# Gated feed-forwards on one core: up-projections as two by two blocks with seven products

## What is computed

```python
D_FF = ((8 * D_MODEL // 3 + 127) // 128) * 128        # 2816
def swiglu_ffn(h, w_in, w_out):                       # w_in 1024 x 5632, w_out 2816 x 1024
    gate, up = jnp.split(h @ w_in, 2, axis=-1)
    return (jax.nn.silu(gate) * up) @ w_out
# in each layer: x = x + 0.5 * swiglu_ffn(rms_norm(x, g), ...), at the start and at the end
```

## Time and profile before

| what | value |
|---|---|
| median of 3 runs | 2511.85 us (2510.24 to 2515.91) |
| the profiled execution's own time | 2515.61 us |
| its span, first to last instruction | 2513.8 us |
| mean granted TensorE clock | 0.982 |
| TensorE busy (matmul) | 2414.4 us, 96% |
| VectorE busy | 588.0 us, 23% |
| ScalarE busy | 356.4 us, 14% |
| matmuls of line 1966 (up) | 615.9 us |
| matmuls of line 1980 (down) | 308.6 us |

### The profile page before, as it was taken

One profiled execution on the slowest core, in us unless ns is written; L12 is line 12 of the kernel. 1 busy time (PEld: TensorE's weight loads), 2 busy tenths in 40 slices (PEclk: granted clock), 3 DMA queues, 4 the chain that ended last, 5 costly groups with the idle time before them and its releaser, 6 DMA issues. The chain is left out here.

```text
span 2513.8 us, 29170 instructions
## 1 busy us (share of the span) xinstructions
PE 2414.4 (96%) x12476; PEld 1658.3 (66%) x12476; DVE 588.0 (23%) x1204; ACT 356.4 (14%) x668; POOL 44.1 (2%) x75
## 2 busy tenths in 40 slices
PE   7999979999999899999999999999999999999998
PEld 4778744444444577778676677777777867667775
DVE  2888221111111200022551110010002164211001
ACT  1123121111111100012213110000001221311000
POOL 1000000000000100000000000000000000000000
PEclk8999979999999999999999999999999999999999
DMA  9565649999999644452322144444445232214442
GB/s 382 222 261 224 240 104 376 422 421 422 422 423 422 232 139 155 157 189 100 131 89 101 51 143 150 151 167 134 150 151 214 76 141 106 95 55 144 150 150 84
DMA packets 176135, 499.46 MB, mean 199 GB/s; under 512 B 7193, under 2 KB 99625, under 8 KB 146097
## 3 DMA queue, kind: packets, MB, share of 16 engines
q1 hardware_dynamic: 172224, 481.23, 51.0%
q0 software_dynamic: 3680, 16.43, 2.2%
q10 hardware_dynamic: 144, 0.52, 0.1%
HBM read 491.34 MB, written 6.82 MB: 198 GB/s over the span
## 5 line engine op out<-in xcount | busy, mean ns | idle before, releaser
L1966 PE MATMUL bank<-xT,ring 128*128 128x256 f32 x2816 | 615.9, 379 | 0.0
L1966 PEld LDWEIGHTS bank<-xT,ring 128*128 128x128 f32 x2816 | 535.1, 190 | 87.9 <-issue 17.2
L1980 PE MATMUL bank<-ring,fh 128*128 128x512 f32 x704 | 308.6, 592 | 0.0
L1980 PEld LDWEIGHTS bank<-ring,fh 128*128 128x128 f32 x704 | 133.8, 190 | 151.3 <-issue 149.2
L2620 DVE TENSOR_TENSOR fs<-bank,R 128x512 f32<-128x512 f32 x44 | 30.4, 692 | 771.1 <-PE bank L1966 771.1
L2015 PE MATMUL bank<-xT,ring 128*128 128x256 f32 x704 | 152.6, 379 | 0.0
L835 PE MATMUL bank<-xT,ring 128*128 128x256 f32 x640 | 143.8, 385 | 2.8 <-ACT xT L279 2.8
L2015 PEld LDWEIGHTS bank<-xT,ring 128*128 128x128 f32 x704 | 133.4, 190 | 18.0
L2418 ACT ACTIVATE fs<-fs 128x512 f32<-128x512 f32 x44 | 27.7, 630 | 800.9 <-DVE fs L2620 800.9
L835 PEld LDWEIGHTS bank<-xT,ring 128*128 128x128 f32 x640 | 122.9, 193 | 22.0 <-ACT xT L279 2.9
L1370 PE MATMUL bank<-ring,xg 128*64 128x512 f32 x512 | 114.4, 594 | 7.6 <-DMA ring<-in_w 7.6
(11 more groups left out here) (433 smaller groups left out, 2215.1 us busy)
## 6 DMA issues: line engine op xcount, KB each, us to landing
ring<-in_w SPq DMA_DIRECT2D x128, 1024.0 KB, 18.6
ring<-in_ffn_w_in SPq DMA_DIRECT2D x88, 1024.0 KB, 7.7
ring<-in_first_pieces SPq DMA_DIRECT2D x33, 2048.0 KB, 12.2
more<-in_w SPq DMA_DIRECT2D x64, 1024.0 KB, 19.7
ring<-in_ffn_w_out SPq DMA_DIRECT2D x44, 1024.0 KB, 4.9
ring<-in_w_mix_in SPq DMA_DIRECT2D x12, 2048.0 KB, 8.8
ring<-in_xattn_w_kv SPq DMA_DIRECT2D x8, 2048.0 KB, 10.5
ring<-in_w_mix_out SPq DMA_DIRECT2D x4, 2048.0 KB, 9.7
```

The lines of the kernel that those rows point to most:

```text
L1966: last = nc.tensor.matmul(bank[2 * par + u][:, c * SEQ:(c + 1) * SEQ], w[:, k, m:m + P], xT[:, k, :], start=(k == 0), stop=(k == KD - 1))
L1980: last = nc.tensor.matmul(bank[4 + 2 * half + t][:, :], fh[:, par, c * SEQ + t * P:c * SEQ + (t + 1) * P], w[:, c, half * 512:(half + 1) * ...
```

## The change

The two by two block form of the product: with x cut into two halves of tokens by two halves of the inner dimension, and the 512 columns of a weight piece cut into gate and linear half by the same halves of the inner dimension, seven block products in place of eight give the result, at the price of sums of blocks of x (4, once a feed-forward, into `Sx`), sums of weight blocks (4 a group, into `Tw`) and sums of products (7 a group, into `part` and `whole`). Each product is 4 matmuls of 128 x 128 by 256 columns. This holds for the groups 1 to 10; group 0 (`up_first`) is the plain product as 16 matmuls of 512 columns.

x is now the stationary operand, so the hidden values come out with the token on the partition. The scale by 1/rms is then a number per partition in ScalarE's silu, and `R`, `spread_rstd` and `take_spread` go from the feed-forwards. But the down-projection wants them transposed: TensorE does four transposes a group into bank 3 (`turned`, in the middle of the down-projection before), and ScalarE copies the bank to `fh`.

VectorE makes the sums of the weight blocks of group g+1 between its steps for group g (`combine_first` to `combine_fourth` in `hidden(g)`). The first waits for both transfers of up-piece g+1. `sync2` is not changed. Three banks hold the seven products, so TensorE's third, fourth, fifth, sixth and seventh product of a group each wait for VectorE or ScalarE. The names of the products, in order: P1, P2, P6, P5, P7, P3, and the last (counted by `hid_up`).

```diff
-                up(0, 0)
-                up(1, 1)
-                down(0, 0, start=True)
...
+                def up(g, i=None):
                     turn = 0 if i is None else i
                     s = wait_piece2(pe, j0 + 2 * g, l, turn)
                     w = slot_w(s, KD, 512)
...
+                    product(0, lambda k: xT[:, k, first], lambda k: w[:, k, gate]).then_inc(ffn_prod, 1)
+                    product(1, lambda k: xT[:, 4 + k, first], lambda k: w[:, 4 + k, gate]).then_inc(ffn_prod, 1)
+                    pe.wait_ge(hid_g, sums(f, g - 1, "weights", i))
+                    product(2, S(2), T(2)).then_inc(ffn_prod, 1)
+                    if g == 1:
+                        turned(0)
+                    pe.wait_ge(ffn_copied, copied(f, g, "P1", i))
+                    product(0, S(1), T(1)).then_inc(ffn_prod, 1)
+                    pe.wait_ge(hid_g, sums(f, g, "gate1", i))
+                    product(1, S(3), T(3)).then_inc(ffn_prod, 1)
+                    pe.wait_ge(hid_g, sums(f, g, "P1+P6", i))
+                    product(2, S(4), lambda k: w[:, 4 + k, linear]).then_inc(ffn_prod, 1)
+                    pe.wait_ge(ffn_copied, copied(f, g, "P5", i))
+                    product(0, lambda k: xT[:, 4 + k, second], T(4)).then_inc(hid_up, 1)
...
+                        if half == 1 and g < FB - 1:
+                            turned(g + 1, i)
...
+                def combine_first(g, i=None):
+                    turn = 0 if i is None else i
+                    s = wait_piece2(dve, j0 + 2 * g, l, turn)
+                    dve.wait_ge(up_full[s], (up_count(l, n, g) + turn) * 16)
+                    w11, w12, w21, w22 = blocks_of(g)
+                    T = Tw[:, g % 2]
+                    st(nc.vector.tensor_tensor(T[:, 0], w12, w11, ALU.subtract))
...
+                    dve.wait_ge(ffn_prod, prod(f, g, "P2", i))
+                    dve.wait_ge(ffn_copied, copied(f, g, "P1", i))
+                    add(whole[:, 0, :], ps[1], P1).then_inc(hid_g, 1)
+                    if g < FB - 1:
+                        combine_first(g + 1, i)
+                    dve.wait_ge(ffn_prod, prod(f, g, "P6", i))
+                    add(U2, ps[2], P1).then_inc(hid_g, 1)
+                    if g < FB - 1:
+                        combine_second(g + 1)
+                    dve.wait_ge(ffn_copied, copied(f, g, "P5", i))
+                    dve.wait_ge(hid_g, sums(f, g, "P1+P6", i))
+                    st(add(V, P5, U2))
+                    dve.wait_ge(ffn_prod, prod(f, g, "P7", i))
+                    st(add(U3, ps[1], U2))
+                    st.sync()
+                    st(add(whole[:, 2, :], P5, U3))
+                    dve.wait_ge(ffn_prod, prod(f, g, "P3", i))
+                    st(add(whole[:, 1, :], ps[2], V))
+                    if g < FB - 1:
+                        combine_third(g + 1)
+                    dve.wait_ge(hid_up, UP_MOE + per_piece(f, 1, g, 1, i))
+                    add(whole[:, 3, :], ps[0], U3).then_inc(hid_g, 1)
+                    st.sync()
+                    dve.wait_ge(hid_silu, per_piece(f, 2, g, 2, i))
+                    nc.vector.scalar_tensor_tensor(out=hh[:, :, :], in0=fs[:, :, :], scalar=0.5, in1=whole[:, 1:3, :],
+                                                   op0=ALU.mult, op1=ALU.mult).then_inc(hid_h, 1)
+                    if g < FB - 1:
+                        combine_fourth(g + 1)
```

More of the change, by code:

```diff
@@ L1759, in build, with nth, prod, copied @@
         FB = NGRP
+        N_PROD, N_COPIED, N_SUMS = 2 + 7 * (FB - 1), 1 + 3 * (FB - 1), 4 * (FB - 1)
+        def nth(f, per, first, each, g, k, i):
+            count = f * per + k if g < 2 else f * per + first + each * (g - 2) + k
+            return count if i is None else i * (2 * each) + count
+        def prod(f, g, name, i=None):
+            order = ("P1", "P2", "P6", "turned0", "P5", "P7", "P3", "turned") if g == 1 else (
+                "P1", "P2", "P6", "P5", "P7", "P3", "turned")
+            k = 1 if name == "first" else order.index(name) + (2 if g == 1 else 1)
+            return nth(f, N_PROD, 9, 7, g, k, i)
+        def copied(f, g, name, i=None):
+            order = ("P1", "h0", "P5", "h") if g == 1 else ("P1", "P5", "h")
+            return nth(f, N_COPIED, 4, 3, g, order.index(name) + 1, i)
+        def sums(f, g, name, i=None):
+            order = ("gate1", "P1+P6", "gate2", "weights")
+            k = 1 if g == 0 else order.index(name) + (2 if g == 1 else 1)
+            return nth(f, N_SUMS, 5, 4, g, k, i)
+        def per_piece(f, each, g, k, i=None):
+            count = (f * FB + g) * each + k
+            return count if i is None else i * (2 * each) + count
         MATS = [("KK", 0, "B", 0), ("B", 0, "KK", 0), ("KK", 1, "B", 1), ("B", 1, "KK", 1),
@@ L1787, in four, with up_count @@
             return t[:, 4 * e:4 * e + 4, :]
+        def up_count(l, n, g):
+            first = 0 if n == 0 else (FB // 2 if g % 2 == 0 else (FB + 1) // 2)
+            return l * FB + (first + g // 2 + 1)
         def wait_piece2(eng, j, l, turn=0):
@@ L1947, in ffn, with up_first, turned @@
                 j0 = (J_FFN1, J_FFN2)[n]
-                def up(g, par, i=None):
+                def up_first():
+                    s = wait_piece2(pe, j0, l)
+                    w = slot_w(s, KD, 512)
+                    pe.wait_ge(up_full[s], up_count(l, n, 0) * 16)
+                    for t in range(NT):
+                        for k in range(KD):
+                            if t == 0:
+                                chunk_ready(pe, l, 3 * n, k)
+                            last = nc.tensor.matmul(bank[4 + t][:, :], xT[:, k, t * P:(t + 1) * P], w[:, k, :],
+                                                    start=(k == 0), stop=(k == KD - 1))
+                        last.then_inc((ffn_prod, hid_up)[t], 1)
+                def turned(g, i=None):
+                    pe.wait_ge(hid_h, per_piece(f, 1, g, 1, i))
+                    for c in range(2):
+                        for t in range(NT):
+                            last = nc.tensor.transpose(bank[3][:, c * SEQ + t * P:c * SEQ + (t + 1) * P],
+                                                       hh[:, t, c * P:(c + 1) * P], eye)
+                    last.then_inc(ffn_prod, 1)
+                def up(g, i=None):
                     turn = 0 if i is None else i
@@ L1954, in up @@
                     w = slot_w(s, KD, 512)
[L1956 to L1968, removed]
@@ L1969, in up, with product @@
-                    last.then_inc(hid_up, 1)
-                def down(g, par, i=None, start=False, stop=False):
+                    pe.wait_ge(up_full[s], (up_count(l, n, g) + turn) * 16)
+                    gate, linear = slice(0, SEQ), slice(SEQ, 2 * SEQ)
+                    first, second = slice(0, P), slice(P, SEQ)
+                    def product(b, lhs, rhs):
+                        for k in range(4):
+                            last = nc.tensor.matmul(bank[b][:, 0:SEQ], lhs(k), rhs(k), start=(k == 0), stop=(k == 3))
+                        return last
@@ L1986, in down @@
                     last.then_inc(hid_down, 1)
-                up(0, 0)
-                up(1, 1)
-                down(0, 0, start=True)
-                with pe.Fori(0, 4) as i:
[L1992 to L1998, removed]
+                up_first()
+                up(1)
+                down(0, start=True)
+                up(2)
+                down(1)
+                with pe.Fori(0, 4) as i:
+                    for g in (3, 4):
+                        up(g, i)
+                        down(g - 1, i)
+                down(10, stop=True)
             def project(l, m):
                 if m == 7:
-                    pe.wait_ge(r_ready, l * 3 + 2)
+                    pe.wait_ge(r_ready, l + 1)
                 elif m >= 8:
@@ L2413, in ffn, with copy, silu, turned @@
                 gained_by_act(act, l * 4 + (4 + 3 * n), gain)
[L2414 to L2426, removed]
+                act.wait_ge(rstd_ready, l * 4 + (5 + 3 * n))
+                def copy(dst, src):
+                    nc.scalar.activation(dst, src, ACT.Copy).then_inc(ffn_copied, 1)
+                def silu(t, src):
+                    nc.scalar.activation(fs[:, t, :], src, ACT.Silu, scale=rstd[:, t:t + 1]).then_inc(hid_silu, 1)
+                def turned(g, i=None):
+                    act.wait_ge(ffn_prod, prod(f, max(g, 1), "turned" if g else "turned0", i))
+                    copy(fh[:, g % 2, :], bank[3][:, :])
+                def hidden(g, i=None):
+                    act.wait_ge(ffn_prod, prod(f, g, "P1", i))
+                    copy(part[:, 0, :], bank[0][:, 0:SEQ])
+                    if g == 1:
+                        turned(0)
+                    act.wait_ge(ffn_prod, prod(f, g, "P5", i))
+                    copy(part[:, 1, :], bank[0][:, 0:SEQ])
+                    act.wait_ge(hid_g, sums(f, g, "gate1", i))
+                    silu(0, whole[:, 0, :])
```

(33 more changed lines are left out.)

52 lines of the change are left out of this document (46 added, 6 removed).

## The result

| | before | changed |
|---|---|---|
| median | 2513.88 us (4 runs, 2510.24 to 2517.44) | 2691.32 us (4 runs, 2690.78 to 2691.59) |
| span of the profiled execution | 2513.8 us | 2689.7 us |
| mean granted TensorE clock | 0.982 | 0.951 |

The change is slower: the ratio is 1.0706, with a 95% interval of 1.0687 to 1.0724. The forecast was 2650 us, in a range from 2600 to 2695.

What follows compares the result with a forecast made beforehand. TensorE was taken as the bound, busy 2414.4 of 2513.8 us. Terms -69.1 - 1.7 + 20.6 + 147.2 + 10.2 + 31 = +138.2 on 2515.61 gave 2653.8, stated as 2650 us; range 2600 to 2695.

Steps and rivals of the forecast that it cites:

- The products: Up-projections of groups 1 to 10, four feed-forwards: each loses one of eight block products, 40 x 1.727 = -69.1 us.
- The transposes: Four new TensorE transposes a group, 0.117 us each: 176 x 0.117 = +20.6 us.
- The stall in rounds 2 to 9: Sixth product 4.60 us late, its sum queued on VectorE behind the wait for the next up-piece: 32 x 4.60 = +147.2 us.
- The stall in up(1): Group 1's up-projection, piece landing at 9.87 us: sixth product starts at 11.64 against 9.10, 4 x 2.54 = +10.2 us.
- The clock: TensorE's granted clock falls after two stalls in three, at 1.3 us each: 24 x 1.3 = +31 us.
- - 1.7: The spread's two 128-column matmuls go from the four feed-forwards: 4 x 2 x 0.216 = -1.7 us.
- weight loads that would stand bare behind waits: Rival: 0.19 us loads bare in 7 products of 40 groups, up to 53 us, some 2690 to 2700 us; chance 0.06.
- every stall costs clock: Rival: the clock falls in all 36 stalls at 1.72 us, 62 us, giving 2681 us; chance 0.20.
- faster: Rival: both halves of the next up-piece land by 6.86 us, VectorE's wait is hidden, -50.2 us, 2462 us; chance 0.07.
- New waits that are met cost nothing: TensorE's five new waits in a group: nothing taken where their producer is early.

## Why the prediction was right, point by point

- **The products (-69.1).** Right. With no stall in the way an up-projection takes 12.08 us (894.59 to 906.67 in the run with the sums last), for 13.81: 1.73 a group.
- **The transposes (+20.6).** Right to 1.4 us: 44 x 0.437 = 19.2.
- **The stall in rounds 2 to 9 (+147.2).** Right in its place, its releaser and its length. I had 4.60 us. The idle time is 137.1 us in 32 stalls, 4.28 each, and it is counted from 0.16 us behind the preceding product's place, so the product is 4.44 late: 142 us. Both conditions were shown one by one, by the order of the queue and by the place of the sum.
- **The stall in up(1) (+10.2).** Too high: 1.08, 1.02, 1.83 and 2.08 us of idleness, 6.7 in all with the 0.16. I had put the transfer's 8.9 us from the profile before; in the changed kernel it is over in about 7.6 (issue at 874.25, VectorE goes at 881.97). The issue stands as I had it, 0.98 us behind the start of up(1) (873.27) for 0.97.
- **The clock (+31).** This is the term that was mis-sized: it measured 74.6 us, 2.4 times as much. I took two falls in three at 1.3 us. The clock fell in all 32 long stalls and in one of the four short ones, and a fall cost 2.3 us on average (1.4 to 3.0 in the 32): the two products behind took 4.95 to 6.56 us where they take 3.56 at full clock. My two prices came from a place with small tiles, where the whole loss was 1.72 us, and from one where the clock was low already when the up-projection began, so that the row shows only the end of it (0.87). The mean of the two was no estimate of a fall between dense matmuls. And I read the fall after 4.5 us of idleness ahead of the mixture as a length that 4.6 us would pass only in part of the rounds, while stops of 2.5 us have now been enough in most cases of one kernel. The two products behind a stop also take 0.10 us more even at full clock (3.56 for 3.45), 3.8 us in 36.
- **Together.** -69.1 - 1.7 + 19.2 + 142.1 + 6.7 + 3.8 + 74.6 = 175.6, against 175.9 between the two profiled spans; the four feed-forwards alone are 175.3 us longer. Nothing is left over.
- **The range.** That 2691 lies within it is in part luck. Its upper end of 2695 was 2681, with a fall in each stall at my price, and some 14 us for weight loads that would stand bare behind waits. The run with the sums last shows nothing of that second cost (below); what filled its place was falls dearer than I had them. The forecast itself was 41 us too low: the clock was worth 44 us more than forecast, the two stalls 9 less.

The rival "every stall costs clock" (2681 us) named the case that came, and the measured 2691 is above it, since its price of 1.72 us was too low as well. The rule of the Trainium skill ("TensorE: Matmul & The Clock Gate", HAM oscillation), that a wait for a transfer in each pass of a loop can throttle the array in each pass, agrees with the trace here, where the wait reaches TensorE by way of VectorE: 32 of 32. In the run with half as many matmuls, where TensorE mostly stood for 2.5 us at the same place, it was 7 of 36. The rival "faster", by which the pieces would be in time, gave 2462 us, and the runs that put them in time measured 2464 to 2471: its price was right, its condition was not met by the change as it was written. New waits that are met cost nothing: in the run with the sums last the view of TensorE's waits has no line of the feed-forwards' products or transposes, and the round of 19.39 us is 20.68 less one product plus the transposes (20.68 - 1.73 + 0.44 = 19.39).

## What to carry to other kernels

When another engine begins to read what TensorE alone read before, look up at what time it asks and what stands ahead of the transfer in its queue: a piece that was 9 us early for TensorE was 7 us late for VectorE, and one line's order in the queue was worth 220 us. Put a step that waits for a transfer behind everything on its engine that somebody else is waiting for. And price a stop of TensorE that comes back in every round with the clock that it may lose behind it, here half as much again as the stop itself.

## What was not expected of the hardware

Two things. First, the clock. A stop of 4.0 to 5.5 us behind dense work let it fall 32 times of 32. One of some 2.5 us did so 28 times of 32 in one kernel and 7 times of 33 in another, where one of 3.67 us held. One of 0.6 to 2.1 us never did in 36 of the run with eight matmuls in the stall, but once, at 2.08 us, in the changed kernel, and once, at 2.10 us, with the queue's order changed. Behind a stop of 4.0 to 5.5 us the low clock lasted, by an estimate from the time lost (twice 1.4 to 3.0 us), through 2.8 to 6 us of work.

Second, a two-operand step of VectorE on 1,024 columns, else 1.23 us, took 4.51 us twice in the profile of the changed kernel, once in the first feed-forward of each layer, each time beside a step of GpSimd on 2,048 columns:

```profile
862.62 3.63 POOL L1958 TENSOR_TENSOR gm<-memT,lc 128x2048 f32<-128x2048 f32 x1
862.82 4.51 DVE L2745 TENSOR_TENSOR Tw<-ring 128x1024 f32<-128x1024 f32 x1
...
867.36 1.23 DVE L2751 TENSOR_TENSOR Tw<-ring,Tw 128x1024 f32<-128x1024 f32 x1
```

```profile
1772.09 4.17 POOL L1958 TENSOR_TENSOR gm<-memT,lc 128x2048 f32<-128x2048 f32 x1
1772.83 4.51 DVE L2751 TENSOR_TENSOR Tw<-ring,Tw 128x1024 f32<-128x1024 f32 x1
```

The profiles of all seven variants of the change show the same two, so it came 16 times of 16, and each ended 1.07 or 1.08 us after the step of GpSimd. That is close to the 1.15 us from one such step's start to the next, as if VectorE had begun only when GpSimd was done. It lay under up_first and cost nothing; no run here set the two steps apart, so the cause is left open.
